# A hybrid decoder layer on one core: the attention's query blocks from the last to the first, eight projection units woven between them, and three small edits

## The reference: what is computed

```python
z = rms_norm(x) @ w_in          # q, k, v, gate_a, qi, ki, wi, glu_a, glu_b, gate_c
q = rms_norm(zq); k = rms_norm(zk); u = glu_a * sigmoid(glu_b)
# sparse attention, 8 heads x 64, 1024 prompt rows in blocks of 128 queries
score = sum_h wi[t,h] * relu(qi[t,h] . ki[s])        # causal
idx = top_k(score, 256)
p = softmax(q . k[idx] / 8 + rel_bias[bucket(t - idx)])
attn = p @ v[idx]
# the same for 8 sample rows against a paged cache of 8192 keys each, keys and values gathered
conv = silu(layer_norm(causal_depthwise_conv31(u)))
y = x + concat(attn * silu(gate_a), conv * silu(gate_c)) @ w_out
```

## Time and profile before

| what | us |
|---|---|
| median of three runs | 1066.73 (1063.25 to 1067.66) |
| the profiled execution, its time | 1068.22 |
| its span, first to last instruction | 1066.4 |
| TensorE busy | 948.5 (89%) |
| VectorE busy | 705.9 (66%) |
| ScalarE busy | 378.1 (35%) |
| mean granted TensorE clock | 0.926 |

### The profile page before, as it was taken

The page is one execution under the profiler, slowest core; times in us unless marked ns, Lnnn a source line. Parts: engine busy times, 40 slices in busy tenths (PEclk is TensorE's granted clock), DMA queues, the critical chain, the costliest instruction groups (busy, mean ns, idle before and its releaser), DMA issues.

```text
span 1066.4 us, 11429 instructions
## 1 busy us (share of the span) xinstructions
PE 948.5 (89%) x3914; PEld 520.4 (49%) x3914; DVE 705.9 (66%) x1662; ACT 378.1 (35%) x837; POOL 85.3 (8%) x90
## 2 busy tenths in 40 slices
PE   3999999945899999999998999694569988999998
PEld 2866666623243444666643334442235555764443
DVE  5306996999897755888868889956766656451111
ACT  6310111101566666889701010312523555461000
POOL 0200111000352000000000000001210012000000
PEclk9889999986999999999999889897559999899999
DMA  8360002200473212101020000005311122000222
GB/s 286 109 237 1 1 7 75 81 0 0 158 232 92 101 40 64 46 21 60 0 100 20 21 20 11 1 0 215 97 42 50 51 61 80 2 1 22 69 79 69
DMA packets 35322, 69.82 MB, mean 65 GB/s; under 512 B 9617, under 2 KB 11961, under 8 KB 35257
## 3 DMA queue, kind: packets, MB, share of 16 engines
q1 hardware_dynamic: 28097, 43.93, 12.1%
q0 software_dynamic: 7168, 25.17, 7.4%
HBM read 58.46 MB, written 11.11 MB: 65 GB/s over the span
## 4 chain that ended last, share of the span: by engine, by line
PE 73%; DVE 18%; ACT 4%; issue 2%; DMA 2%; SPq 0%; DVEq 0%; ACTq 0%; POOLq 0%
PE ps L485 68%; DVE ctmp L1258 8%; PE ps L488 5%; DVE ct L1232 1%; ACT PTs L931 1%; DMA xn<-in_x_prompt 1%; DVE pv L1460 1%; DMA KVr<-in_cache_k,idx 1%; ACT uT L1110 1%; DVE LB L1461 1%; DVE Pm L1698 0%; DVE LG L1587 0%; ACT relu L1048 0%; DVE prod L1585 0%; ACT sqj L944 0%
## 5 line engine op out<-in xcount | busy, mean ns | idle before, releaser
L485 PE MATMUL ps<-xT,W 128*128 128x344 f32 x960 | 286.6, 461 | 0.0
L485 PEld LDWEIGHTS ps<-xT,W 128*128 128x128 f32 x960 | 185.4, 194 | 99.4 <-issue 8.4
L485 PE MATMUL ps<-W,xT 128*128 128x512 f32 (+3 forms) x576 | 215.5, 533 | 1.2 <-ACT relu L1048 1.2
L1258 DVE SCALAR_TENSOR_TENSOR ctmp<-uT,chw,ctmp 128x1024 f32<-128x1024 f32 x116 | 152.0, 1310 | 4.1
L485 PEld LDWEIGHTS ps<-W,xT 128*128 128x128 f32 (+1 forms) x576 | 95.2, 185 | 114.2 <-issue 113.8
L1078 ACT ACTIVATE sgj<-SC,candn 128x1024 bf16<-128x1024 f32 (+3 forms) x128 | 114.5, 896 | 8.6 <-DVE candn L1364 6.3
L1675 DVE TENSOR_TENSOR resid<-resid,ps 128x512 f32<-128x512 f32 (+1 forms) x18 | 12.3, 685 | 88.7 <-PE ps L485 88.5
L485 PE MATMUL ps<-kT,qT 64*128 64x512 f32 (+3 forms) x192 | 45.0, 576 | 27.6 <-DVE mx L1698 24.2
L1123 ACT ACTIVATE nsq<-ps 128x512 f32<-128x512 f32 (+1 forms) x18 | 10.7, 596 | 164.8 <-DVE nss L1473 122.0
L931 ACT ACTIVATE PTs<-ps 128x512 f32<-128x512 f32 (+3 forms) x96 | 43.0, 480 | 71.7 <-PE ps L488 71.6
L1137 ACT ACTIVATE Pm<-Pm,mx 128x128 f32<-128x128 f32 (+7 forms) x64 | 49.5, 773 | 52.9 <-DVE mx L1701 52.1
(11 more groups left out here) (309 smaller groups left out, 1082.5 us busy)
## 6 DMA issues: line engine op xcount, KB each, us to landing
W<-in_w_in SPq DMA_DIRECT2D x8, 2048.0 KB, 8.6
xn<-in_x_prompt SPq DMA_DIRECT2D x8, 512.0 KB, 7.7
W<-in_w_out SPq DMA_DIRECT2D x1, 4096.0 KB, 15.1
resid<-in_x_prompt SPq DMA_DIRECT2D x16, 256.0 KB
out<-resid SPq DMA_DIRECT2D x16, 256.0 KB
out<-V SPq DMA_DIRECT2D x8, 256.0 KB
out<-zN SPq DMA_DIRECT2D x8, 256.0 KB, 2.0
bias_rows<-tprow SPq DMA_DIRECT2D x1, 1536.0 KB, 9.6
```

The source lines that it names most:

```text
L485: return nc.tensor.matmul(out, lhsT, rhs, start=start, stop=stop)
L1258: ins = vec.scalar_tensor_tensor(conv[:, c, :] if j == CW - 1 else acc_, src, chw[:, c, j:j + 1], acc_, ALU.mult, ALU.add)
```

## The change

The steps run over the blocks 7 to 0. `Y` runs over the row tiles 7 to 1, then the sample rows, then 0; its first eight units are woven in from step 34, two matmuls a step, and ten follow. The q tiles are normed from 7 to 0. All decode pieces move to later step numbers: key tiles to steps 2 to 17, their query rows into bank 7. `scores` of a block waits for the k tiles of all blocks up to it.

The three small edits: the bias table by one matmul and one copy, whose eight rows the write to DRAM repeats 128 times; the sign of q, bias and masks turned round, so that VectorE's minimum is itself the exponential's bias and the sign instruction goes; the rank rows in the order `RANKED`, where four in a row read four different groups of 32 partitions.

```diff
-    lnsq = sb("lnsq", [P, 4, SEQ], F32, rQK)[:, :, 512:SEQ]
+    lnsq = sb("lnsq", [P, 4, SEQ], F32, rQK)[:, :, 0:512]
-    tprow = sb("tprow", [P, H, FW], F32, rV)
+    tprow = sb("tprow", [H, FW], F32, rV)
-    vrow = sb("vrow", [P, 512], F32, rSC)
+    vrow = sb("vrow", [P, 512], F32, rSC + 12800)
-    NORMED = [(g, t) for g in ("k", "q") for t in range(NT + 1)]
+    NORMED = [("k", t) for t in range(NT + 1)] + [("q", t) for t in list(range(NT - 1, -1, -1)) + [NT]]
+    RANKED = [(b, tl) for tl in range(2) for par in range(2) for b in range(par, NB, 2)]
-    STEPS = [(i, h) for i in range(NT) for h in range(H)]
+    STEPS = [(i, h) for i in range(NT - 1, -1, -1) for h in range(H)]
-    V_AT = [34, 38, 42, 46]
-    Y = [(t, half) for t in [0, 1, NT] + list(range(2, NT)) for half in range(2)]
-    YEARLY = 4
-    Y_FROM, Y_RATE = 16, 2
-    Y_ADD = [max(22, Y_FROM + (8 * u + 7) // Y_RATE) for u in range(YEARLY)]
+    V_AT = [37, 41, 45, 49]
+    Y = [(t, half) for t in list(range(NT - 1, 0, -1)) + [NT, 0] for half in range(2)]
+    YEARLY = 8
+    Y_FROM, Y_RATE = 34, 2
+    Y_ADD = [Y_FROM + (8 * u + 7) // Y_RATE + 1 for u in range(YEARLY)]
...
-        for h in range(H):
-            o = begin(("tp", h), f"b{4 + h % 2}")
-            mm(o[:, 0:FW], rb[0:NBK, h:h + 1].broadcast_to([NBK, P]), oneh[:, :]).then_inc(plan.fill_sem(("tp", h)), 1)
+        o = begin("tp", "b4")
+        mm(o[0:H, 0:FW], rb[0:NBK, 0:H], oneh[:, :]).then_inc(plan.fill_sem("tp"), 1)
...
-            b, tl = s // 2, s % 2
+            b, tl = RANKED[s]
...
-            wait(*plan.drained(("tr", "k", i)))
+            for kb in range(i + 1):
+                wait(*plan.drained(("tr", "k", kb)))
...
-            if n < 16 and n % 2 == 0:
-                b = n // 2
+            if 2 <= n < 18 and n % 2 == 0:
+                b = n // 2 - 1
                 wait(zn_ready, len(NORMED))
-                o = begin(("qb", b), ("b1", "b3")[b % 2])
+                o = begin(("qb", b), "b7")
...
-                wait(*(plan.drained("mixa") if t == NT else (at_ready, t + 1)))
+                wait(*(plan.drained("mixa") if t == NT else (at_ready, NT - t)))
...
-                     scale=1.0 if g == "k" else HD ** -0.5)
+                     scale=1.0 if g == "k" else -HD ** -0.5)
...
-            act.wait_ge(nmx_ready, n + 1)
-            nc.scalar.activation(Pm[:, n % 3, 0:L], Pm[:, n % 3, 0:L], ACT.Exp, bias=mx[:, n % 4, 1:2],
+            act.wait_ge(*plan.drained(("S", n)))
+            nc.scalar.activation(Pm[:, n % 3, 0:L], Pm[:, n % 3, 0:L], ACT.Exp, bias=mn[:, n % 4:n % 4 + 1], scale=-1.0,
                                  accum_out=sums[:, n:n + 1]).then_inc(exp_done, 1)
...
-            vec.tensor_tensor_reduce(out=Pm[:, n % 3, 0:L], in0=s, in1=m, scale=1.0, scalar=-3.0e38, op0=ALU.add, op1=ALU.max,
-                                     accum_out=mx[:, n % 4, 0:1]).then_inc(plan.drain_sem(("S", n)), 1)
-            v.wait_ge(*plan.drained(("S", n)))
-            vec.tensor_scalar(mx[:, n % 4, 1:2], mx[:, n % 4, 0:1], -1.0, None, ALU.mult).then_inc(nmx_ready, 1)
+            vec.tensor_tensor_reduce(out=Pm[:, n % 3, 0:L], in0=s, in1=m, scale=1.0, scalar=3.0e38, op0=ALU.add, op1=ALU.min,
+                                     accum_out=mn[:, n % 4:n % 4 + 1]).then_inc(plan.drain_sem(("S", n)), 1)
...
-                g.wait_ge(nmx_ready, 4 * H)
+                for n in (H - 2, H - 1):
+                    g.wait_ge(*plan.drained(("S", n)))
...
-        for h in range(H):
-            sp.wait_ge(*plan.drained(("tp", h)))
-        sp.dma_start(tpd.rearrange("h (p x) -> p h x", p=P), tprow[:]).then_inc(tp_out, 16)
+        sp.wait_ge(*plan.drained("tp"))
+        sp.dma_start(tpd.rearrange("h (p x) -> h p x", p=P), tprow[:, :].unsqueeze(1).broadcast_to([H, P, FW])).then_inc(tp_out, 16)
```

More of the change, by code:

```diff
@@ L802, in values, with spread_sums @@
                 last.then_inc(pv_done, 1)
-        def spread_sums(i):
-            wait(row_sums, i + 1)
-            o = begin(("rr", i), t_unit())
+        def spread_sums(j):
+            wait(row_sums, j + 1)
+            o = begin(("rr", NT - 1 - j), t_unit())
             for h in range(H):
@@ L810, in spread_sums @@
                 last = mm(o[r:r + 64, h // 2 * P:(h // 2 + 1) * P], rs8[:, h:h + 1].broadcast_to([P, HD]), ident)
-            last.then_inc(plan.fill_sem(("rr", i)), 1)
+            last.then_inc(plan.fill_sem(("rr", NT - 1 - j)), 1)
         def small_transposes(tag, src, sem_v, n_in, width):
@@ L966, in _ @@
         ki_out(NT - 1)
-        for h in range(H):
-            copy(tprow[:, h, :], pt(("tp", h))[:, 0:FW], ("tp", h))
+        copy(tprow[:, :], pt("tp")[0:H, 0:FW], "tp")
         def sample_row(g, func):
@@ L1147, in probs_out @@
                     if p % 4 == 3:
-                        act.wait_ge(*plan.full(("o", p // 4)))
+                        act.wait_ge(*plan.full(("o", STEPS[2 * p][0])))
                     else:
@@ L1388, in mask @@
             link(vec.scalar_tensor_tensor(s, s, th(j), meq[:, 0:L], ALU.is_gt, ALU.add))
-            last = vec.tensor_scalar(s, s, -1.0, -MASKED, ALU.add, ALU.mult)
+            last = vec.tensor_scalar(s, s, -1.0, MASKED, ALU.add, ALU.mult)
             if j < 5:
@@ L1642, in decode_piece, with invert_sums, attn_out @@
                                   ALU.mult).then_inc(plan.drain_sem("mixa"), 1)
-        def invert_sums(i):
-            v.wait_ge(exp_done, (i + 1) * H)
-            vec.reciprocal(rs8[:], sums[:, i * H:(i + 1) * H]).then_inc(row_sums, 1)
-        def attn_out(i):
+        def invert_sums(j):
+            v.wait_ge(exp_done, (j + 1) * H)
+            vec.reciprocal(rs8[:], sums[:, j * H:(j + 1) * H]).then_inc(row_sums, 1)
+        def attn_out(j):
+            i = NT - 1 - j
             g = gaT[:, :, i * P:(i + 1) * P]
@@ L1686, in _ @@
             m = sc(i) if i >= 2 else (cmask[:, P:2 * P] if i == 0 else cmask)
-            if h == 2 and i >= 1:
-                invert_sums(i - 1)
-            if h == 4 and i >= 1:
-                attn_out(i - 1)
+            if h == 2 and n >= H:
+                invert_sums(n // H - 1)
+            if h == 4 and n >= H:
+                attn_out(n // H - 1)
             v.wait_ge(*plan.full(("S", n)))
             s = pair_of(("S", n), L)
-            link(vec.tensor_tensor(s[:, L - bw:L], s[:, L - bw:L], TP[:, h, BAND - bw:BAND], ALU.add))
+            link(vec.tensor_tensor(s[:, L - bw:L], s[:, L - bw:L], TP[:, h, BAND - bw:BAND], ALU.subtract))
             if n >= 3:
@@ L1711, in _ @@
         attn_out(NT - 1)
-        for u in range(YEARLY, len(Y)):
+        for u in range(sum(1 for a in Y_ADD if a < len(STEPS)), len(Y)):
             residual(u)
@@ L1754, in _ @@
         g.wait_ge(pool_step, 2)
[L1755 removed]
+        pool.affine_select(out=cmask[:, P:2 * P], in_=cmask[:, P:2 * P], compare_op=ALU.is_ge, fill=-MASKED, base=0,
                            pattern=[[-1, P]], channel_multiplier=1).then_inc(pool_step, 1)
@@ L1771, in _ @@
             g.wait_ge(zn_out[k], zn_stored(16 + k))
-            g.wait_ge(*plan.full(("tr", "q", NT - 2 + k)))
+            g.wait_ge(*plan.full(("tr", "q", k)))
         g.wait_ge(zn_ready, len(NORMED))
```

76 lines of the change are left out of this document (37 added, 39 removed).

## The result

The changed kernel took a median of 1074.43 us in ten runs (1068.72 to 1091.53), the kernel before 1067.01 beside it: a ratio of 1.0075, 95% interval 1.0047 to 1.0104. The ratio leaves out two of the ten, 1091.53 and 1088.53, which lie over 1.5% above the fastest. That is slower by 0.7%, where 0.6% faster was predicted; the time lies inside the range and the sign is wrong.

A forecast was written before the change was run, and what follows sets the result against it. It saw idle TensorE in attention's first stretch and a TensorE-only tail at the end. From 729.6 us its steps reached 838.9, 892, 1000 and 1072.2; minus 12 for small edits gave 1060 us, against 1066.73, range 1044 to 1078.

The forecast's parts named there:

- The small edits, -12: Bias table by one matmul, 10 us gained; regrouped rank rows, 2 us; turned sign, hidden by TensorE; together -12 us.
- steps 1 and 2: Start of attention: first scores 2.4 us later, pair 1's scores at 737.9; pairs 1 and 2 take 28 us by ScalarE's Silu.
- step 3: Pairs 3 to 7 at 12.4 us a cycle, query row and half clock included: 62 us, plus 11 for pair 8.
- rival A: Pairs 3 to 8: the clock holds, cycles of 10.5 instead of 12.4 us, 1049 us in all; chance 0.27.
- rival B: Pairs 3 to 8: the clock stays low, cycles of 17.5 us, +31 us, 1091 us in all; chance 0.15.
- Pairs 9 to 15, 53 us: Seven pairs at 5.1 us, 36, plus 17 of work formerly under the Y units: 53 us, bounds 45 to 60.
- step 5: Blocks 3 to 0 and the drain, bound by TensorE with eight woven units: 108 us.
- Attention 32.8: Blocks 3 to 0: attention by pair about 3.1, 2.5, 1.7 and 1.0 us, times four, 32.8 us.
- Units 55.2: Blocks 3 to 0: eight woven projection units at 6.9 us each, 55.2 us.
- Sums 4.1: Blocks 3 to 0: spreading sums takes 4.1 us.
- My sign of being wrong: Wrong if the first 18 steps take under 95 us, or blocks 3 to 0 well over 110 (too many units).
- Rival C: Table's write on half the engines takes 19 us; if glua's weights land 10 us late, 1070 us; chance 0.14.

The follow-up runs named there:

- e1: Kernel before with the three small edits alone (order, weave and decode places as before): 1056.63 us, ratio 0.9884.
- e4: Changed kernel with four projection units of Y woven in instead of eight: 1079.48 us.
- e12: Changed kernel with query row right behind its pair's scores, both Silu pieces in step 1, scores issued head by head: 1036.43 us, ratio 0.9731.
- e14: Kernel before with small edits, query row behind its pair's scores, Silu pieces early, scores head by head: 1041.08 us, ratio 0.9774.
- e3: Changed kernel with the query-row matmul moved from the pair's end to right behind the pair's scores: 1046.56 us, ratio 0.9787.
- e13: Changed kernel with eight dummy score matmuls filling TensorE's wait for the previous odd head, pairs 2 to 8: 1071.18 us, ratio 1.0063 to the kernel before.
- e11: Changed kernel, query row still at the pair's end, scores issued head by head, each waiting for its own tile only: 1085.09 us.
- e10: Changed kernel with sixteen dummy score matmuls in TensorE's wait for the previous odd head, pairs 2 to 8: 1085.81 us.

## Why the prediction was wrong, step by step

Compared are the instants of the forecast less 12 us with the changed kernel's. The forecast counts from the start of one pair's scores to the next, so these rows are TensorE's: the scores of pairs 1, 3, 9 and 16, and the first matmul of the tail.

```profile
726.03 3.78 PE L486 MATMUL ps<-kT,qT 64*128 64x512 f32 x8 [5.92 <-DVE mn L1700]
755.10 3.78 PE L486 MATMUL ps<-kT,qT 64*128 64x512 f32 x8 [3.33 <-DVE mn L1700]
828.12 2.26 PE L486 MATMUL ps<-kT,qT 64*128 64x512 f32 x8 [3.06 <-DVE mn L1700]
879.59 1.67 PE L486 MATMUL ps<-kT,qT 64*128 64x512 f32 x4 [3.04 <-DVE mn L1700]
998.83 3.70 PE L486 MATMUL ps<-W,qT 128*128 128x512 f32 x8
```

1. *The small edits, -12*: about 11 came. The table gave 10 of it. The rank rows were to give 2 and gave 0.5 in e1 (first to last read of the ranks 44.0 us, before 44.5) and 1.5 in the turned order (569.8 to 612.8): the matmuls did fall to 1.13 and 2.00 for four records, but each group still waited for VectorE's reads, 0.9 to 1.6 us in the changed kernel and once 3.3 in e1.
2. *First scores and pairs 1 and 2, steps 1 and 2*: the first scores were to be full at 720.0, S(0) is at 720.2; pair 1's scores forecast at 725.9, found at 726.0; pair 3's at 753.9, found at 755.1. The chain by ScalarE's Silu took 29.1 us for 28.
3. *The cycle of 12.4 us in pairs 3 to 8, step 3*: right in its mechanism and in its sum. From 755.10 to 828.12 it is 73.0 us, for the forecast's 62 and 11, with the 3.3 us wait and the scores and transposes at the low clock. That it fits to 0.1 us is luck: pair by pair, by VectorE's starts, it went 12.9, 12.7, 12.9, 9.7, 11.7 and 11.4. Neither rival A (10.5 each) nor rival B (17.5) is what the rows show: the mean clock of steps 0 to 17 is 0.79.
4. *Pairs 9 to 15, 53 us*: 51.5 (828.12 to 879.59). Up to here the forecast is under 1 us off, with +1.1 and -1.5 in it.
5. *Blocks 3 to 0, "bound by TensorE", 108 us*: this is the step that failed. They are bound by TensorE (116.5 of 118.0 us busy in the window above, over my 95%), but from pair 16's scores to the tail it is 119.2 us, and those 11 us are the difference between 1060 and the 1071.4 of this profile. The next rows are from its start and its middle:

```profile
881.19 1.33 PE L489 MATMUL ps<-Cc,Pm 128*128 128x128 f32 x5
883.15 1.30 PE L489 MATMUL ps<-Cc,Pm 128*128 128x128 f32 x5 [0.62 <-ACT PTs L932]
884.38 2.40 PE L486 MATMUL ps<-PTs,V 128*64 128x128 f32 x20
886.71 1.19 PE L486 MATMUL ps<-kT,qT 64*128 64x512 f32 x4
...
888.85 1.31 PE L486 MATMUL ps<-PTs,V 128*64 128x128 f32 x20
...
947.52 3.70 PE L486 MATMUL ps<-W,qT 128*128 128x512 f32 x8
951.15 1.09 PE L486 MATMUL ps<-Cc,rs 128*64 128x128 f32 x16
...
959.92 6.39 PE L486 MATMUL ps<-W,uT 128*128 128x512 f32 x8
...
1002.37 3.60 PE L486 MATMUL ps<-W,uT 128*128 128x512 f32 x8
1005.80 3.60 PE L486 MATMUL ps<-W,qT 128*128 128x512 f32 x8
```

   Two terms were mis-sized above all (all by the starts in TensorE's timeline, waits left out). *Attention 32.8*: the scores, transposes and value products take 41.1 us. I had counted sixteen pairs of blocks 3 to 0, but the pipeline lags, and behind S(32) come the transposes of the last pair of block 4 and the value products of its last two, larger ones: 5.5 us from 881.19 to 886.71, with a wait of 0.6 in it, and 1.25 more at 888.85, together 6.1; the other 2.1 are the first scores at half clock (1.60 us for 1.1) and pairs of blocks 1 and 0 that took 1.8 and 1.2 us and not 1.7 and 1.0. (The four prices times four make 33.2 and not 32.8; that is rounding.) *Units 55.2*: 59.0, without the half clock. Between attention pieces half a unit takes 3.63 us (947.52 to 951.15), and 3.83 in the five that another piece splits, in the tail 3.43 (1002.37 to 1005.80). *Sums 4.1*: five blocks' sums are spread in this stretch, not four, 1.0 more, and small products that had no price take 0.4. On the other side the half clock behind the mixing (6.3 us for 3.6) cost 2.7 and was priced at 3.5, and the waits are 1.5 and not 3. That is 8.3 + 3.8 + 1.0 + 0.4 - 0.8 - 1.5, the 11.2 us.
6. *Tail, 72.2*: 72.6 (998.83 to 1071.4).

My sign of being wrong, blocks 3 to 0 well over 110 us, did come, but the reason that I gave with it, too many woven units, isn't what e4 shows: with four units the kernel is 5 us slower still. The forecast was -6.7 us and +7.4 was measured; of these 14 us 11.4 show in the span, nearly all of them in this step, and the rest lies between the profiled executions and the medians.

So the mechanism that I named as the place "where the change gives back" was there at its forecast price, and the sign hung on the smaller sums of step 5.

Rival C is half true: the write of the table was slow, by far slower than I had it, and the time didn't move. Its rows in the changed kernel, the issue of the write and of the load that waits for it (the start in us twice, last but one column):

```profile
L1835 SPq DMA_DIRECT2D bias_rows<-tprow x1: 850/850/850, 49.8 to 49.8; - x1
L1837 SPq DMA_DIRECT2D TP<-bias_rows x1: 367/367/367, 89.6 to 89.6; - x1
```

and a window in between (DMA share and GB/s are the last two columns):

```profile
64.00:72.00 8.00, 8.00 (x29) 5.31 (x28) 0.00 (x0) 0.46 (x1) 0.79 (x1) 1.00 0.46 50
```

By the issue of the load it takes 39.8 us, where it took 9.6 (and the load was issued at 68.1), in the window from 64 to 72 us at a DMA share of 0.46, about half of the sixteen engines' time, at 50 GB/s. That agrees with the rule cited from the Trainium skill, DMA: Bandwidth & Descriptors, Rules for kernel authors. My 19 us took half the engines at the old rate each; the trace shows twice that, and what makes the other factor of two is open. It is hidden because the weights of `glua` were issued ahead of it and the table is read 630 us later; TensorE shows no wait there.

The price of each part, then, by these runs: small edits about -11; all from S(32) on -16.4, of which the second four woven units are 3 to 5 (e4) and the rest, small blocks in place of large ones, isn't taken apart; steps 0 to 17 +32.1. Of these 32, the row's place is 19.9 (it costs the turned order 31.0 us and the old one 11.1), and 12.1 stay when the row is early in both (79.2 against 67.1). The order as such is worth nothing until the row, the Silu pieces and the first head's scores have been moved, and 4 to 5 us with them (e12 against e14).

## What to carry to other kernels

When an order of work is turned so that small, latency-bound pieces fall beside large blocks, look first for the piece that the turned order makes everybody wait for, here one matmul of 1.1 us issued at the end of a pair and read by an engine that queues the next mask behind it; moving it was worth four times what the whole change was to bring. In a forecast for a pipelined loop, cut the stretch where the bound engine changes its work and not where another engine's step begins: what lags from the block before is paid in the next stretch. And price pieces woven between others by a woven row, not by one from a run of their own. When a chain makes an engine wait, try first what e3 did; filling the wait, as in e13, gave 7 us in its stretch and nothing in the total.

## What was not expected of the hardware

- A wait of 3.3 us costs TensorE more than itself: at a granted clock of 0.50 behind it, eight score records take 3.36 us, and sixteen transpose records 3.38 at 0.62, instead of 1.8 and about 2.1. It isn't the same in each pair: behind 3.2 us the same scores once took 2.83 (804.37), and behind 2.2 us 1.77 (793.12). With eight dummy records in the wait the clock stays at 1.00 and the pair takes 10.35 us, not 12.9.
- Eight score records of two heads, on rows 0 to 63 and 64 to 127 in turn, take 1.77 us; four of one head alone take 1.77 as well (e11). The two halves of the rows work side by side, and they do so too when the heads are issued one behind the other and both tiles are free: 1.78 us for the eight in e12, whose two heads start 0.01 us apart by the trace. What stops it is a wait between the two.
- The first profile of the changed kernel had its key projections of the indexer at half clock from 34 to 61 us (a mean of 0.52), with the same instructions as in the others. A row of it, and the same work in the second profile:

```profile
51.63 3.53 PE L486 MATMUL ps<-W,xT 128*128 128x72 f32 x16
```

```profile
40.90 1.90 PE L486 MATMUL ps<-W,xT 128*128 128x72 f32 x16
```

  It put the first tap at 95.76 us. S(0) came 13.9 us later than in the second profile. What granted or refused the clock there isn't settled; none of the other profiles of this study has it. The times of e10 and e11 spread widely too (15 and 30 us), and their medians are to be taken with care.
